# Weighting a head's values key tile by key tile for all four query tiles at once

## The chip, the cores and the metric

The kernel runs on one core of a Trainium2 chip. The metric is device time in microseconds for one execution. Three runs of the kernel before gave 3425.62, 3419.9 and 3424.49 us, median 3424.49. The profiled execution took 3425.8 us.

## The reference

Three transformer blocks over 512 tokens of width 1024, all in float32: two of the first kind (two gated feed-forwards around a mixer) and one of the second (16 meta tokens go ahead, one feed-forward). A mixer projects its input, runs attentions as branches, and merges them through gates. What the change touches is the last step of each attention, the product of the probabilities with the values:

```
p = jax.nn.softmax(sc, axis=-1)
a = p[:, :, 0] - lam * p[:, :, 1]
return jnp.einsum('bhqk,bhke->bhqe', a.astype(v.dtype), v)          # differential ("C"), 4 heads of 128
...
out = jnp.einsum('bkgnqj,bknjd->bkgnqd', p.astype(v.dtype), vb)     # sliding window ("B"), 8 heads of 64
out = jnp.einsum('bhrcij,bhrijd->bhrcd', p, vg)                     # neighbourhood ("A"), 8 heads of 64
...
o = jnp.einsum('bnhgqk,bnkhd->bnqhgd', p, v_band)                   # second block: causal window ("S")
o = jnp.einsum('bhqk,bkhd->bqhd', p, v)                             # second block: forgetting ("F")
```

Each attention is over 4 query tiles of 128 tokens. In C a query tile sees all 4 key tiles, in B its own and the neighbours, in S the one before and its own, in F all up to its own. Key tile 0 (S and F) holds the 16 meta tokens.

## The kernel before

Five programs, one for each engine, are written out by hand and meet at counted semaphores. Activations lie transposed in SBUF, weights are streamed in, split into a high and a low float32r part (`wh` by ACT, `wl` by DVE), and every dense product is three matmuls. Stages run in the order v = 0 to 7: feed-forwards at 0, 2, 3, 5 and 7, mixers at 1 and 4 (attentions C, B, A) and at 6 (S, F).

An attention (`ATT`, L427) is a list of units. Unit u is head x = u // 4 and query tile j = u % 4 + 1, with its key tiles. C has 16 units, the others 32. All engines loop over n (L1096 on TensorE, L1627 on ACT, L2342 on DVE). In round n TensorE does, in this order:

- the scores of unit n (`PS<-stk` in the rows);
- a piece of other dense work, the filler (`PS<-uh,wh` and its like), as much as the stage's quota says (`Fill`, L358, L379, L390): most rounds have one piece of six matmuls or more, in B rounds 24 and 31 have none, in F rounds 19, 21, 24, 26, 28 and 30 have none;
- `turned` (L1152): the transposes of the probabilities of unit n - lag into bank 6 or 7 (`PS<-ident,tmp`, L1171, key tile 0 at L1164). The lag is 3, in C 2. Below this is called turn u;
- `weighted` (L1174) for unit n - lag - 2: one fp32 matmul of 128 columns for each key tile, `V` as weights and the transposed probabilities `PT` as the moving operand (`PS<-PT,V`). In F units j = 1 and j = 2 go together.

DVE takes the maximum and the bias of unit n (L2297, in F L2276) and normalises unit n - 1. ACT takes the exponential of unit n (L1555) and copies turn u from PSUM to `PT` (L1588, `PT<-PS`; below: copy u). `PT` has room for the four units of one head. Where the filler's quota is zero or the attention is F, ACT makes copy u first and the exponential of unit n after it, otherwise the exponential comes first:

```
                    idle = n >= len(fill.quota) or fill.quota[n] == 0
                    if 0 <= u < A.n and (idle or st == "F"):
                        turned(v, st, u)
                    if n < A.n:
                        exponential(v, st, n)
```

The sum of a head lies in bank 3 (in B and S bank 3 or 2), from where ACT takes it after unit j = 4.

Of the kernel before, what the change touches and what calls it, by code (L numbers as in the profile page):

```python
# [15 lines left out]
P = 128  # L16
# [401 lines left out]
class Units:  # L418
# [8 lines left out]
ATT = {  # L427
    "C": Units("C", [(x, j, [1, 2, 3, 4]) for x in range(4) for j in range(1, 5)], 2, 4),
    "B": Units("B", [(x, j, [i for i in (j - 1, j, j + 1) if 1 <= i <= 4]) for x in range(8) for j in range(1, 5)], 3, 8),
    "A": Units("A", [(x, j, [1, 2]) for x in range(8) for j in range(1, 5)], 3, 8),  # L430
    "S": Units("S", [(x, j, [j - 1, j]) for x in range(8) for j in range(1, 5)], 3, 8),
    "F": Units("F", [(x, j, list(range(j + 1))) for x in range(8) for j in range(1, 5)], 3, 8),
}
# [14 lines left out]
def build(nc, T, OUT, CUM, VAL):  # L448
    JOBS, PIECES, CUTS, FILLS = plan()
    ctx = ExitStack()  # L450
    with ctx:
# [7 lines left out]
        def sb(name, shape, dt, offset):  # L459
            return nc.alloc_sbuf_tensor_at(name, list(shape), dt, offset=offset)  # L460
# [36 lines left out]
        V = sb("V", [P, 5, 512], F32, XV)  # L497
        PT = sb("PT", [P, 5, 512], F32, XV + 10240)
# [23 lines left out]
        def bank(b, c0=0, c1=512):  # L522
            return PS[:, 512 * b + c0:512 * b + c1]
# [26 lines left out]
        def slots_of(st, p):  # L550

            if st in "CAF":
                return pair_slots(p)
            return [2 * (p % 2), 2 * (p % 2) + 1], ([(4, 5), (6, 7)] if st == "B" else [(8, 9), (10, 11)])

        def pair_of(st, x):
            return (x, None) if st == "C" else (x // 2, x % 2)

        def v_cols(st, x):
            if st in "BS":  # L560
                return slice(0, P)
            return slice(P * x, P * x + P) if st == "C" else slice(P * (x // 2), P * (x // 2) + P)

        def tiles(v):
            return [0, 1, 2, 3, 4] if v == 6 else [1, 2, 3, 4]
# [4 lines left out]
        def tokens(j):  # L570
            q0 = 0 if j == 0 else X0 + P * (j - 1)
            return slice(q0, q0 + P)

        def grid(ap):

            return ap.rearrange("p (r c) -> p r c", c=64)
# [145 lines left out]
        class S:  # L722
            mm = Signal(ctx.enter_context(nc.semaphore("s_dense")))
# [3 lines left out]
            st = Signal(ctx.enter_context(nc.semaphore("s_sums")))  # L727
# [3 lines left out]
            pt = Signal(ctx.enter_context(nc.semaphore("s_probabilities_t")))  # L731
# [7 lines left out]
            x = [Signal(ctx.enter_context(nc.semaphore(f"s_x{i}"))) for i in range(8)]  # L739
# [39 lines left out]
        def tensor_program(E):  # L779
            e, held = E.e, {}  # L780

            def take(b, signal, *event):

                if b in held:
                    E.wait_ge(*held[b])
                held[b] = (signal, *event)

            def mm(out, lhs, rhs, start, stop):
                return e.matmul(out, lhs, rhs, start=start, stop=stop, skip_group_check=True)  # L789
# [306 lines left out]
            def attention(v, st, fill):  # L1096
                A = ATT[st]
                jobs = iter(fill.jobs)
                now, left = iter(()), [0]

                def filler(steps):
                    nonlocal now
                    for _ in range(steps):
                        if left[0] == 0:
                            job = next(jobs)
                            now, left[0] = dense(job, v, "o" if job.kind == "br" else "u"), job.kt // 2 * len(job.chunks)
                        next(now)
                        left[0] -= 1

                for n in range(A.n + A.lag + 4):  # L1110
                    if n < A.n:
                        x, j, kts = A.units[n]
                        p, hh = pair_of(st, x)
                        E.wait_ge(S.dv, "stk", ("q", v, st, p))
                        E.wait_ge(S.kd[0 if st in "BS" else p % 2], "halves", ("k", v, st, 0 if st in "BS" else p))
                        qs, ks = slots_of(st, p)
                        if st == "C":
                            for s in range(2):
                                b = (2, 4, 5)[(2 * n + s) % 3]
                                take(b, S.ex, "exp", v, st, n, s)  # L1120
                                scores(v, st, n, b, qs[s], *ks[s], S.sc, (st, v, n, s))
                        else:
                            b = 4 if st == "F" and j == 4 else 4 + n % 2
                            take(b, S.sx, "max", v, st, n)
                            if st == "F" and j == 4:
                                take(5, S.sx, "max", v, st, n)
                            scores(v, st, n, b, qs[hh], *ks[hh], S.sc, (st, v, n))
                    if n < len(fill.quota):
                        filler(fill.quota[n])
                    if st == "S" and n == 1:  # L1130
                        values_turned(v, "S")
                    u = n - A.lag
                    if 0 <= u < A.n:
                        turned(v, st, u)
                    u = n - A.lag - 2
                    if 0 <= u < A.n:
                        if st != "F":
                            weighted(v, st, u)
                        elif A.units[u][1] > 1:
                            for i in (u - 1, u) if A.units[u][1] == 2 else (u,):  # L1140
                                weighted(v, st, i)
                    u = n - A.lag - 4 + 1
                    if st == "C" and 0 <= u < A.n and A.units[u][1] == 4:
                        x = A.units[u][0]
                        b = 6 + u % 2
                        take(b, S.an, "c_sum", v, x)
                        E.wait_ge(S.an, "c_out", v, x)
                        for q in range(4):
                            i = mm(bank(b, q, q + 1), oblf[:, x, X0 + P * q:X0 + P * q + P], ones[:, 0:1], True, True)
                        i.then_inc(*S.st.up(("c_sum", v, x)))  # L1150

            def turned(v, st, u):  # L1152

                A = ATT[st]
                x, j, kts = A.units[u]
                E.wait_ge(S.id, "id")
                E.wait_ge(S.ex if st == "F" else S.sx, "p", v, st, u)
                b = 6 + u % 2
                take(b, S.pt, "pt", v, st, u)
                if 0 in kts:  # L1160
                    b0, c0 = (6 + u % 2, 384) if st == "S" else (2, 0)
                    if st == "F":
                        take(2, S.pt, "pt0", v, st, u)
                    i = e.transpose(bank(b0, c0, c0 + P)[0:16, :], scores_of(st, u, 0, 16), ident[:, :])  # L1164
                    i.then_inc(*S.tp.up(("pt0", v, st, u)))
                for a in kts:
                    if a > 0:
                        k0, k1 = key_range(a)
                        if st == "A":
                            k0, k1 = P * (a - 1), P * a  # L1170
                        i = e.transpose(bank(b, P * (a - 1), P * a), scores_of(st, u, k0, k1), ident[:, :])  # L1171
                i.then_inc(*S.tp.up(("pt", v, st, u)))

            def weighted(v, st, u):  # L1174

# [110 lines left out]
        def scalar_program(E):  # L1286
# [301 lines left out]
            def turned(v, st, u):  # L1588

                A = ATT[st]  # L1590
                x, j, kts = A.units[u]
                if u >= len(A.units) // (4 if st == "C" else 8):
                    E.wait_ge(S.pv, st, v, u - len(A.units) // (4 if st == "C" else 8))
                big = [i for i in kts if i > 0]
                b = 6 + u % 2
                if 0 in kts:
                    b0, c0 = (b, 384) if st == "S" else (2, 0)
                    E.wait_ge(S.tp, "pt" if st == "S" else "pt0", v, st, u)
                    E.wait_ge(S.dv, "zero")
                    act(PT[0:16, 0, P * (j - 1):P * j], bank(b0, c0, c0 + P)[0:16, :], ACT.Copy).then_inc(  # L1600
                        *S.pt.up(("pt0", v, st, u)))
                a, z = big[0], big[-1] + 1
                to = 2 if st == "A" else 0
                E.wait_ge(S.tp, "pt", v, st, u)
                act(PT[:, a + to:z + to, P * (j - 1):P * j],
                    bank(b, P * (a - 1), P * (z - 1)).rearrange("p (i q) -> p i q", q=P), ACT.Copy).then_inc(
                    *S.pt.up(("pt", v, st, u)))
# [1344 lines left out]
```

## Time and profile before

| | us |
|---|---|
| median of three runs | 3424.49 |
| profiled execution | 3425.8 |
| its span, first to last instruction | 3423.9 |
| TensorE busy in the span | 3348.1 |
| VectorE busy | 2413.3 |
| ScalarE busy | 1687.4 |
| TensorE clock granted, share of full speed | 0.996 |

The span is almost all TensorE. A matmul's record in the trace covers its way through the array, and records overlap, so that the rate of a series is read from the starts or from the length of a whole series, not from one record's length. An fp32 matmul has two records (the 592 products of probabilities with values give 1184), a float32r matmul one.

### The profile page before, as it was taken

How to read it: one execution, taken by the hardware profiler on the slowest of the kernel's cores; microseconds unless marked ns; L12 is line 12 of the kernel's file. 1: busy time of each engine (PE TensorE's matmuls, PEld its weight loads, DVE VectorE, ACT ScalarE, POOL GpSimd, SP SyncE). 2: the span in 40 equal slices, each digit the busy share in tenths (PEclk: the TensorE clock that was granted, in tenths of full speed). 3: DMA queues.
4: the chain of work that ended last, by engine and by line, in shares of the span. 5: the costliest groups of instructions: out<-in, count | busy, mean ns of one | idle time of the engine just before them, and what ended most of it. 6: DMA issues, size and time to landing. Idle time of an engine off the chain costs nothing.

```text
span 3423.9 us, 51537 instructions
## 1 busy us (share of the span) xinstructions
PE 3348.1 (98%) x20344; PEld 2954.7 (86%) x20344; DVE 2413.3 (70%) x3919; ACT 1687.4 (49%) x3057; POOL 816.6 (24%) x607
## 2 busy tenths in 40 slices
PE   8999999999999999999999999999999999999998
PEld 6999887878889998999887878889988888888997
DVE  6878665756687778777766656687768676649775
ACT  4545454635454445445454544454446374334443
POOL 1533110121043413432111021053400001205331
PEclk9999999999999999999999999999999999999999
DMA  3333343253223332333433253223322322322332
GB/s 130 108 96 110 104 107 84 69 142 90 86 93 102 102 106 74 105 105 112 109 82 93 69 148 93 74 92 102 109 95 91 90 79 69 111 84 85 102 107 81
DMA packets 116673, 332.79 MB, mean 97 GB/s; under 512 B 18888, under 2 KB 19656, under 8 KB 116432
## 3 DMA queue, kind: packets, MB, share of 16 engines
q1 hardware_dynamic: 104112, 306.82, 28.9%
q0 software_dynamic: 12320, 22.66, 3.3%
q8 instruction: 162, 2.65, 0.3%
q14 instruction: 79, 0.65, 0.1%
HBM read 306.23 MB, written 4.21 MB: 91 GB/s over the span
## 4 chain that ended last, share of the span: by engine, by line
PE 84%; DVE 9%; ACT 2%; DMA 2%; issue 1%; POOL 1%; SPq 0%; DVEq 0%; POOLq 0%; ACTq 0%
PE PS L789 82%; DVE wl L1839 2%; PE PS L1171 2%; DVE bl L2023 1%; ACT wh L1290 1%; DMA raw<-in_gu 1%; DVE gx L1987 1%; DMA raw<-in_win 1%; POOL ws L2700 0%; DVE bf L2003 0%; DVE tmp L1911 0%; DVE tmp L1968 0%; DVE h L1914 0%; DVE b L2003 0%; DVE b L2004 0%
## 5 line engine op out<-in xcount | busy, mean ns | idle before, releaser
L1839 DVE TENSOR_TENSOR wl<-raw,wh 128x1024 fp32r<-128x1024 f32 (+2 forms) x635 | 790.9, 1249 | 300.0 <-ACT wh L1290 293.3
L1290 ACT ACTIVATE wh<-raw 128x1024 fp32r<-128x1024 f32 (+2 forms) x635 | 553.9, 878 | 413.5 <-PE PS L789 387.6
L789 PE MATMUL PS<-bh,wh 128*128 128x256 f32 x2520 | 710.1, 282 | 6.8 <-DVE h L1936 2.9
L789 PE MATMUL PS<-bh,wl 128*128 128x256 f32 x2520 | 708.0, 281 | 0.0
L789 PE MATMUL PS<-bl,wh 128*128 128x256 f32 x2520 | 707.9, 281 | 0.0
L789 PE MATMUL PS<-uh,wh 128*128 128x512 f32 (+2 forms) x1656 | 616.4, 372 | 24.0 <-DVE ul L1867 16.2
L789 PE MATMUL PS<-uh,wl 128*128 128x512 f32 (+2 forms) x1656 | 606.6, 366 | 0.0
L789 PE MATMUL PS<-ul,wh 128*128 128x512 f32 (+2 forms) x1656 | 604.6, 365 | 0.0
L789 PEld LDWEIGHTS PS<-bh,wh 128*128 128x128 f32 x2520 | 474.8, 188 | 11.6 <-DVE h L1936 3.3
L789 PEld LDWEIGHTS PS<-bh,wl 128*128 128x128 f32 x2520 | 474.8, 188 | 0.6
L789 PEld LDWEIGHTS PS<-bl,wh 128*128 128x128 f32 x2520 | 474.9, 188 | 0.0
L789 PE MATMUL PS<-gx,wh 128*128 128x512 f32 (+1 forms) x1424 | 429.3, 375 | 14.6 <-DVE gx L1987 11.9
L789 PEld LDWEIGHTS PS<-uh,wh 128*128 128x128 f32 x1656 | 313.1, 189 | 82.0 <-DVE wl L1839 15.3
L789 PEld LDWEIGHTS PS<-ul,wh 128*128 128x128 f32 x1656 | 313.3, 189 | 52.4
L789 PEld LDWEIGHTS PS<-uh,wl 128*128 128x128 f32 x1656 | 313.1, 189 | 47.3 <-issue 1.4
L789 PEld LDWEIGHTS PS<-gx,wh 128*128 128x128 f32 x1424 | 261.2, 189 | 69.4 <-DVE gx L1987 14.1
L1839 DVE TENSOR_TENSOR wl<-ws,wh 128x1024 fp32r<-128x1024 f32 x180 | 269.2, 1496 | 34.7 <-ACT wh L1290 34.7
L789 PE MATMUL PS<-gx,wl 128*128 128x512 f32 (+1 forms) x712 | 266.5, 374 | 0.0
L2700 POOL TENSOR_TENSOR ws<-raw 128x512 f32<-128x512 f32 x90 | 124.7, 1386 | 537.4 <-DMA raw<-in_gu 304.7
L1290 ACT ACTIVATE wh<-ws 128x1024 fp32r<-128x1024 f32 x180 | 191.0, 1061 | 114.1 <-PE PS L789 83.4
L1290 ACT ACTIVATE tmp<-PS 128x256 f32<-128x256 f32 (+1 forms) x382 | 146.8, 386 | 161.3 <-PE PS L789 161.0
L2726 POOL DMA_DIRECT2D tmp<-tmp x88 | 69.6, 1324 | 586.3 <-DVE tmp L2230 456.2
(263 smaller groups left out, 5693.7 us busy)
## 6 DMA issues: line engine op xcount, KB each, us to landing
raw<-in_gu SPq DMA_DIRECT2D x220, 512.0 KB, 3.2
raw<-in_win SPq DMA_DIRECT2D x139, 512.0 KB, 3.3
raw<-in_dn SPq DMA_DIRECT2D x80, 320.0 KB, 3.0
raw<-in_dn SPq DMA_DIRECT2D x40, 512.0 KB, 3.6
raw<-in_wbr SPq DMA_DIRECT2D x72, 256.0 KB, 2.7
raw<-in_wout SPq DMA_DIRECT2D x24, 512.0 KB, 3.2
raw<-in_dn SPq DMA_DIRECT2D x40, 256.0 KB, 2.7
raw<-in_wv SPq DMA_DIRECT2D x20, 512.0 KB, 3.2
```

Source lines behind the costliest of these rows:

```text
L789: return e.matmul(out, lhs, rhs, start=start, stop=stop, skip_group_check=True)
L1171: i = e.transpose(bank(b, P * (a - 1), P * a), scores_of(st, u, k0, k1), ident[:, :])
L1290: return e.activation(out, in_, f, scale=scale, **more)
L1839: tt(wl[:, c % 4, 0:n], src, wh[:, c % 4, 0:n], SUB).then_inc(*S.lo.up(("lo", c)))
L1987: tt(lo, tmp[:, 2 + f % 2, X0:TW], hi, SUB).then_inc(*S.dv.up(("g", v, f)))
L2023: tt(bl[:, i, :], b21[:, :] if i == 2 else bf[:, i, :], bh[:, i, :], SUB).then_inc(*S.dn.up(("operand", v, i)))
L2700: tt(ws[:, 0:512], b[:, 0:512], b[:, 512:1024], ADD).then_inc(*S.pl.up(("sum1", p)))
L2726: e.dma_start(tmp[o:o + 32, temp_of(tag), X0:TW], turn_at(turn_of(tag))[a:a + 32, X0:TW], accum_op=ADD).then_inc(*S.rp[turn_of(tag)].land( ...
```

## The change

For every head but the last of C, B, S and F, the products are no longer made unit by unit. A new function `weighted_head` runs once per head, in the round in which the next head's first unit is turned, ahead of that turn. It waits for all four copies of the head and makes one matmul for each key tile, over all query tiles that see it: 4 matmuls of 512 columns in C; of 256, 384, 384 and 256 in B; of 128, 256, 256, 256 and 128 in S; of 512, 512, 384, 256 and 128 in F. On ACT a copy into `PT` waits for the whole head that lay there. Attention A and the last heads are as before.

```diff
@@ -571,6 +571,14 @@
             q0 = 0 if j == 0 else X0 + P * (j - 1)
             return slice(q0, q0 + P)
 
+        def together(st, x):
+
+            return st != "A" and x < ATT[st].units[-1][0]
+
+        def weighed(v, st, u):
+
+            return st, v, u | 3 if together(st, ATT[st].units[u][0]) else u
+
         def grid(ap):
 
             return ap.rearrange("p (r c) -> p r c", c=64)
@@ -1130,10 +1138,12 @@
                     if st == "S" and n == 1:
                         values_turned(v, "S")
                     u = n - A.lag
+                    if 0 < u < A.n and A.units[u - 1][1] == 4 and together(st, A.units[u - 1][0]):
+                        weighted_head(v, st, u - 1)
                     if 0 <= u < A.n:
                         turned(v, st, u)
                     u = n - A.lag - 2
-                    if 0 <= u < A.n:
+                    if 0 <= u < A.n and not together(st, A.units[u][0]):
                         if st != "F":
                             weighted(v, st, u)
                         elif A.units[u][1] > 1:
@@ -1170,6 +1180,29 @@
                             k0, k1 = P * (a - 1), P * a
                         i = e.transpose(bank(b, P * (a - 1), P * a), scores_of(st, u, k0, k1), ident[:, :])
                 i.then_inc(*S.tp.up(("pt", v, st, u)))
+
+            def weighted_head(v, st, u):
+
+                A = ATT[st]
+                x, units = A.units[u][0], A.units[u - 3:u + 1]
+                vc = v_cols(st, x)
+                for t in (tiles(v) if st in "CF" else tiles(v)[-4:][:1] + tiles(v)[:-4]):
+                    E.wait_ge(S.aa, "vv", v, st, t)
+                for i in range(u - 3, u + 1):
+                    if 0 in A.units[i][2]:
+                        E.wait_ge(S.pt, "pt0", v, st, i)
+                    E.wait_ge(S.pt, "pt", v, st, i)
+                b = 3 if st in "CF" else (3, 2)[x % 2]
+                if st == "C":
+                    take(b, S.an, "c_out", v, x)
+                else:
+                    take(b, S.dv, "ol", v, st, x)
+                keys = sorted({a for unit in units for a in unit[2]})
+                for a in keys:
+                    js = [j for _, j, kts in units if a in kts]
+                    c0, c1 = P * (js[0] - 1), P * js[-1]
+                    i = mm(bank(b, c0, c1), V[:, a, vc], PT[:, a, c0:c1], a == keys[0], a == keys[-1])
+                i.then_inc(*S.pv.up((st, v, u)))
 
             def weighted(v, st, u):
 
@@ -1589,8 +1622,8 @@
 
                 A = ATT[st]
                 x, j, kts = A.units[u]
-                if u >= len(A.units) // (4 if st == "C" else 8):
-                    E.wait_ge(S.pv, st, v, u - len(A.units) // (4 if st == "C" else 8))
+                if u >= 4:
+                    E.wait_ge(S.pv, *weighed(v, st, u - 4))
                 big = [i for i in kts if i > 0]
                 b = 6 + u % 2
                 if 0 in kts:
```

The first head of B, TensorE, rounds 7 and 8 (`PS<-ident,tmp` is turn 4, `PS<-stk` the scores of unit 8). Before:

```order
L789 MATMUL PS<-ul,wh 128x512
L1171 MATMUL PS<-ident,tmp 128x128 [waits s_probabilities_t,s_softmax]
L1171 MATMUL PS<-ident,tmp 128x128
L789 MATMUL PS<-PT,V 128x128 x3
L789 MATMUL PS<-stk 128x256 [waits s_softmax,s_dve_dense]
```

and now:

```order
L797 MATMUL PS<-ul,wh 128x512
L797 MATMUL PS<-PT,V 128x256 [waits s_probabilities_t]
L797 MATMUL PS<-PT,V 128x384 x2
L797 MATMUL PS<-PT,V 128x256
L1181 MATMUL PS<-ident,tmp 128x128 [waits s_softmax]
L1181 MATMUL PS<-ident,tmp 128x128
L797 MATMUL PS<-stk 128x256 [waits s_softmax,s_dve_dense]
```

The product of the head stands ahead of turn 4 and waits for copy 3 (`s_probabilities_t`), which was made one round earlier.

The end of B, TensorE, rounds 31 to 34 (scores of unit 31, turns 28, 29 and 30). Before:

```order
L789 MATMUL PS<-stk 128x256 [waits s_softmax]
L789 MATMUL PS<-stk 128x256
L1171 MATMUL PS<-ident,tmp 128x128 [waits s_probabilities_t,s_softmax]
L1171 MATMUL PS<-ident,tmp 128x128
L789 MATMUL PS<-PT,V 128x128 x3
L1171 MATMUL PS<-ident,tmp 128x128 [waits s_probabilities_t,s_softmax]
L1171 MATMUL PS<-ident,tmp 128x128 x2
L789 MATMUL PS<-PT,V 128x128 x2
```

and now:

```order
L797 MATMUL PS<-stk 128x256 [waits s_softmax]
L797 MATMUL PS<-stk 128x256
L797 MATMUL PS<-PT,V 128x256 [waits s_dve_dense,s_probabilities_t]
L797 MATMUL PS<-PT,V 128x384 x2
L797 MATMUL PS<-PT,V 128x256
L1181 MATMUL PS<-ident,tmp 128x128 [waits s_softmax]
L1181 MATMUL PS<-ident,tmp 128x128
L1181 MATMUL PS<-ident,tmp 128x128 [waits s_softmax]
L1181 MATMUL PS<-ident,tmp 128x128 x2
```

Four matmuls of head 6 now stand between the last scores and turn 28; what was weighted after turns 28 and 29 is gone from there.

## Rows read from the trace of the kernel before

**Rows 1.** The page's first part: busy time, share of the span, instructions.
```profile
PE 3348.1 (98%) x20344; PEld 2954.7 (86%) x20344; DVE 2413.3 (70%) x3919; ACT 1687.4 (49%) x3057; POOL 816.6 (24%) x607
```
**Rows 2.** Timeline of TensorE: start us, length us, operation, records; fp32 series only.
```profile
484.66 0.95 PE L789 MATMUL PS<-ones,oblf 128*128 128x1 f32 x8
...
530.06 2.84 PE L789 MATMUL PS<-PT,V 128*128 128x128 f32 x24
...
546.22 1.02 PE L789 MATMUL PS<-tmp,ones 128*128 128x512 f32 x2
```
**Rows 3.** Busy time by window: B of v = 1, S and F.
```profile
597.00:680.00 83.00, 80.02 (x489) 69.77 (x488) 65.68 (x215) 55.84 (x151) 10.73 (x14) 1.00 0.26 70
...
2588.00:2663.00 75.00, 74.59 (x457) 63.99 (x456) 61.62 (x222) 53.95 (x166) 3.23 (x6) 1.00 0.24 78
2728.00:2832.00 104.00, 100.81 (x684) 89.78 (x683) 74.71 (x164) 72.13 (x185) 3.22 (x6) 1.00 0.29 87
```
**Rows 4.** Timeline of TensorE, B of v = 1.
```profile
605.56 0.38 PE L1171 MATMUL PS<-ident,tmp 128*128 128x128 f32 x2
...
608.09 0.38 PE L1171 MATMUL PS<-ident,tmp 128*128 128x128 f32 x2
...
610.36 0.51 PE L789 MATMUL PS<-stk 128*128 128x256 f32 x2 [1.23 <-DVE stk L2248]
...
655.44 0.38 PE L1171 MATMUL PS<-ident,tmp 128*128 128x128 f32 x2
...
671.95 0.38 PE L1171 MATMUL PS<-ident,tmp 128*128 128x128 f32 x2
...
673.08 0.38 PE L1171 MATMUL PS<-ident,tmp 128*128 128x128 f32 x2
...
677.51 0.41 PE L1171 MATMUL PS<-ident,tmp 128*128 128x128 f32 x2 [1.76 <-ACT PT L1290]
```
**Rows 5.** Timeline of ACT, the same stage: copies 3, 19, 27, 28, exponential 31, copy 29.
```profile
608.93 0.36 ACT L1290 ACTIVATE PT<-PS 128x256 f32<-128x256 f32 x1
...
655.02 0.36 ACT L1290 ACTIVATE PT<-PS 128x256 f32<-128x256 f32 x1
...
672.41 0.36 ACT L1290 ACTIVATE PT<-PS 128x256 f32<-128x256 f32 x1
673.56 0.38 ACT L1290 ACTIVATE PT<-PS 128x256 f32<-128x256 f32 x1 [0.79 <-PE PS L1171]
674.00 0.51 ACT L1290 ACTIVATE tmp<-tmp,small 128x256 f32<-128x256 f32 x1
...
676.89 0.47 ACT L1290 ACTIVATE PT<-PS 128x384 f32<-128x384 f32 x1
```
**Rows 6.** Timelines in S: turn 12, copy 11, DVE ahead of it.
```profile
2621.20 0.27 PE L1164 MATMUL PS<-ident,tmp 128*16 128x128 f32 x1
...
2620.84 0.36 ACT L1290 ACTIVATE PT<-PS 128x256 f32<-128x256 f32 x1
...
2618.01 1.39 DVE L2248 TENSOR_TENSOR stk<-tmp,stk 64x512 fp32r<-64x512 f32 x2
```
**Rows 7.** Timeline of TensorE in F: turns 12, 16, 20 and 24.
```profile
2782.11 0.27 PE L1164 MATMUL PS<-ident,tmp 128*16 128x128 f32 x1
...
2792.53 0.27 PE L1164 MATMUL PS<-ident,tmp 128*16 128x128 f32 x1
...
2802.98 0.27 PE L1164 MATMUL PS<-ident,tmp 128*16 128x128 f32 x1
...
2812.51 0.27 PE L1164 MATMUL PS<-ident,tmp 128*16 128x128 f32 x1
```
**Rows 8.** Timeline of ACT in F: copies 19, 23 and 27.
```profile
2800.18 0.73 ACT L1290 ACTIVATE PT<-PS 16x128 f32<-16x128 f32 x2
...
2809.64 0.72 ACT L1290 ACTIVATE PT<-PS 16x128 f32<-16x128 f32 x2
...
2818.72 0.73 ACT L1290 ACTIVATE PT<-PS 16x128 f32<-16x128 f32 x2
```

## The prediction

> **What bounds the kernel now.** I read the page's first part: TensorE is busy 3348.1 us of a span of 3423.9, DVE 70%, ACT 49% [rows 1]. So TensorE sets the time, and what counts is its own work and each moment at which it stands still. Then the windows of the stages that change [rows 3]: in B, S and F TensorE is busy 96%, 99% and 97%, DVE 79%, 82% and 72%, ACT 67%, 72% and 69%. Hardly any stall is there to be won back; a new one is paid in full. Last the timelines around each head's end [rows 4 to 8], for how soon after a turn ACT's copy is ready, since the head's product now waits for the copy one round earlier.
>
> **TensorE's own work.** Before, a series of 24 records of 128 columns is 2.84 us long, a record on its own 0.275: (2.84 - 0.275) / 23 = 0.1115 us a record. One column costs nearly as much: 8 records in 0.95 us, so about 0.10 each. Two records of 512 columns last 1.02 us, one alone 0.592: 0.428 us apart, and 0.428 is 3.84 times 0.1115, not once [rows 2]. So at 128 columns the streaming has all but caught up with the weight load, and a wide matmul saves next to nothing.
>
> Moved are C 6 heads x 16, B 14 x 10, S 7 x 8 and F 7 x 14 matmuls: 390, or 780 records of 128 columns, 87.0 us. New are 150 matmuls. Widths of 256 and 384 are not in the trace as fp32. Bounds: by columns from the 512 row 0.214 and 0.321, by whole 128-column records 0.223 and 0.335. I take 0.216 and 0.322, near the 512 row, as the steps are the same streaming. 38 matmuls of 512 x 2 x 0.428 = 32.5; 35 of 384: 22.5; 56 of 256: 24.2; 21 of 128: 4.7; together 83.9 us. The change saves 3.1 us of TensorE, 1.5 to 3.3 by the bounds. A head's product lasts 3.4 us in C, 2.15 in B, 1.74 in S, 3.0 in F.
>
> For the narrow matmul the Trainium skill ("TensorE: Matmul & The Clock Gate", Back-to-back issue gap) gives a stream of weight loads and matmuls about 81 ns at 128 columns and 131 ns at 512, that is, the load weighs most and width is cheap. By its ratio, 131/81 x 0.1115 = 0.18 us for a 512 record, the estimated saving would be some 40 us, not 3; the trace's 0.428 disagrees.
>
> **The wait that is added, B.** The product of head x needs copy 4x + 3, and everything behind it on TensorE waits with it: turn, scores, filler. TensorE also comes to it sooner, for the products of units before are gone.
> Head 0: turn 3 starts at 605.56 and turn 4 at 608.09; without units 0 and 1 (4 and 6 records, 1.1 us) TensorE would be ready for the product at 607.1 on the old time line. Copy 3 is done at 608.93 + 0.36 = 609.29, as ACT first stacks a query (which waits for a DMA), converts weights and takes the exponential; from a copy's end to TensorE's start 0.15 us pass (676.89 + 0.47 to 677.51) [rows 4, 5]. Stall 2.3 us. The stall of 1.23 at 610.36 goes, its data being there at 610.3 and the scores now later. Net +1.0.
> Head 4: ready at 655.44 less units 15 to 17 (14 records, 1.56) = 653.9; copy 19 ends at 655.38, and can come at most 0.45 earlier, as ACT runs on without a gap there: stall 1.2 us. Head 2 by the same working 0.2. Heads 1, 3 and 5 have their copies ready well ahead (1.3 to 1.7 us before the turn) and stall nothing; their rows, which repeat the pattern, are not shown, here and for the heads named without rows below. The end of B: round 31 has no filler. Turn 27 is at 671.95, its copy over at 672.77, so the product of head 6 starts 0.97 us after the turn and ends at +3.12; turn 28 follows, copy 28 0.48 later, and only then the exponential of unit 31, for in this round ACT copies first: at +4.0. It was at 674.00, +2.05. Everything to the end of B hangs on this exponential: TensorE already waits 1.76 us for copy 29 [rows 4, 5]. So +2.0, and no product left to fill the gap. Sum per layer: 1.0 + 0.2 + 1.2 + 2.0, less six heads' saving 0.47 and less unit 24 (0.45), which the old program has behind it at turn 27 and the new one not: +3.5. Two layers (v = 1 and 4, whose copies lie alike): +7.0 us.
>
> **S.** Always one filler, so exponential first. Turn 12 at 2621.20, copy 11 over at 2621.20, behind DVE, which is busy without a gap since it stacked the next query (2618.01) and cannot hurry [rows 6]. Without units 7 to 9 (12 records, 1.34 us) TensorE is ready at 2619.86, so it stalls 1.5 us. Head 4 has the same pattern, 1.5; head 0 has 0.75; heads 1, 3, 5 and 6 none. The saving is 0.3. The end of S is bound by ACT's copies, and the old program at turn 28 still had units 26 and 27 (0.9 us) to put beside them: 3.75 - 0.3 + 0.9 = +4.3 us.
>
> **F.** ACT always copies first, so the exponential waits through the whole product of the last head. Up to turn 12 the quotas are 2 and 3 and hide it: at turn 12 the new program has made units 10 and 11 too (18 records, 2.0 us), less 0.3 saved: +1.7, to be kept, since from here ACT sets the pace. From turn 20 (2802.98) copy 23 ends 7.38 later (2810.36) with ACT never idle between copy 20 and it; the product then takes 3.0, and turn 24 comes at +10.5 where it came at +9.53: +1.0. From turn 24 copy 27 ends at +6.94, 0.37 of it spare: +9.7 for 8.9, +0.7. From 12 to 16 (10.42) I get +0.75, from 16 to 20 (10.45) nothing, TensorE being last there (copy 19 ends 2800.91) [rows 7, 8]. The tail is ACT's as before. Sum +4.2 us.
>
> **C.** Rounds last 5 to 6 us and copies are ready 3.8 us and more ahead; the rates save 0.4 us a layer, the tail, which is a chain over ACT, gives back the unit 11 that filled it (0.9), and ACT's output comes 0.3 earlier: +0.2 a layer, +0.4.
>
> **Sum.** 7.0 + 4.3 + 4.2 + 0.4 = +15.9 us, on 3425.8 (span and 1.9 around it): 3441.7. The median shown lies 1.3 below the profiled run: 3440. After each attention TensorE goes on with dense work at once, with nothing to absorb this.
>
> **Rivals.**
> 1. The chains give way: DVE and ACT follow TensorE forward where it comes sooner, stalls inside B and S vanish, and only the structural parts stay: the end of B (2.0 less 0.9, twice), F about 2.5, S 0.6. Sum about +6: 3430. For it: DVE is only 82% busy even in S. Against: it is without a gap just ahead of copy 11.
> 2. Not slower, on the other side: the two-round distance was not needed, copies keep ready and the wide matmuls' 3.1 us is all: 3421. It holds if copy 3 and copy 11 end before TensorE is there; against it stand 609.29 and 2621.20. A variant, that weight loads alone set the pace and a record of any width costs the one-column 0.10: 780 x 0.1115 less 300 x 0.10, -57 us, 3367; the 0.428 row rules it out.
> 3. Worse: TensorE's work comes in lumps, so DVE idles through each product and then has 1.88 us a round (61.62 over the window's 33 rounds of 2.29) against TensorE's shortened 1.84 in S; new waits for weights and maxima in every head, 0.5 us in each of 28 heads: +14 on top, 3454.
>
> **Chances.** Forecast 0.55 (own range 3435 to 3446), rival 1 0.2, rival 2 0.09 and its cheap variant 0.01, rival 3 0.15. 0.2% is 6.8 us, about what a measurement can tell. Rival 2 lies within it, rival 1 on its edge (3431.3), half either way: same 0.19, faster 0.01, and 0.80 slower, of which I move 0.01 to faster. The range 3427 to 3450 leaves out the fast cases and the heavy end of rival 3.
>
> **What would show it.** `PS<-PT,V` of 512 columns 0.43 us apart. TensorE idle ahead of `PS<-PT,V` waiting for ACT's `PT`: about 2.3 us at head 0 of B, 1.2 at head 4, 1.5 at heads 2 and 4 of S, 0.5 in late F. At the end of B the exponential of unit 31 some 4 us after turn 27. B's window longer by 3.5 us each, S's by 4.3, F's by 4.2, A's and the feed-forwards' the same. The prediction is wrong if these stalls are absent, or if copies end sooner than on the old time line; and in its sum if 256- and 384-column records are not near 0.22 and 0.32 us.

## The result, and the profile after

The changed kernel takes 3448.38 us, the median of four runs (3443.92 to 3454.84), beside 3424.56 for the kernel before (3419.9 to 3425.62). The ratio is 1.0067, 95% interval 1.0055 to 1.0079: slower by 0.67%. The prediction was 3440, range 3427 to 3450. Five later executions of the same kernel had a median of 3451.61 (below, "The changed kernel again"). The profiled execution of the changed kernel took 3454.84 us, at a mean granted TensorE clock of 0.992; that of before had 0.996.

The page's first part, changed kernel: TensorE has 480 records fewer, as 390 matmuls became 150, and yet is busy 12.5 us longer than in [rows 1]. The lower clock can account for that: leaving out the stretch in which each program ends, this execution has 44 us at half clock and the one of the kernel before has 17, and half of the 27 us between them is 13.6.

```profile
PE 3360.6 (97%) x19864; PEld 2931.0 (85%) x19864; DVE 2420.1 (70%) x3919; ACT 1686.7 (49%) x3057; POOL 813.2 (24%) x607
```

The waits of TensorE, changed kernel (engine, what waited and where, what for: us in all, times, longest). Before, the first of these lines did not reach 1 us, and the other two were 6.7 us (4 times) and 2.4 us (3 times).

```profile
PE PS L797 <- ACT PT L1323: 11.7, 11, 2.5
PE PS L1181 <- ACT PT L1323: 9.1, 8, 2.3
PE PS L1174 <- ACT PT L1323: 6.9, 8, 2.0
```

Together 27.7 us of standing still for ACT's copies where there were 9.4: 18 us more, of which products not left to fill the old waits are a part. (The 9.4 hold 0.3 us of the first line.)

TensorE's timeline, attention B of v = 1, changed kernel (start, length, operation, records, in brackets the idle time before it and its releaser). It answers to [rows 4]: turn 3, the product of head 0, turn 4; the product of head 4 and turn 20; turn 27, the product of head 6, turns 28 and 29, turn 31.

```profile
605.89 0.38 PE L1181 MATMUL PS<-ident,tmp 128*128 128x128 f32 x2
...
610.44 3.77 PE L797 MATMUL PS<-PT,V 128*128 128x256 f32 x8 [2.50 <-ACT PT L1323]
614.05 0.38 PE L1181 MATMUL PS<-ident,tmp 128*128 128x128 f32 x2
...
658.94 2.39 PE L797 MATMUL PS<-PT,V 128*128 128x256 f32 x8 [1.04 <-ACT PT L1323]
661.17 0.38 PE L1181 MATMUL PS<-ident,tmp 128*128 128x128 f32 x2
...
675.82 0.38 PE L1181 MATMUL PS<-ident,tmp 128*128 128x128 f32 x2
...
676.91 2.39 PE L797 MATMUL PS<-PT,V 128*128 128x256 f32 x8 [0.47 <-ACT PT L1323]
679.13 0.71 PE L1181 MATMUL PS<-ident,tmp 128*128 128x128 f32 x5
...
683.39 0.41 PE L1181 MATMUL PS<-ident,tmp 128*128 128x128 f32 x2 [2.29 <-ACT PT L1323]
```

ACT's, the end of the same stage; it answers to the last rows of [rows 5].

```profile
676.45 0.36 ACT L1323 ACTIVATE PT<-PS 128x256 f32<-128x256 f32 x1
679.61 0.38 ACT L1323 ACTIVATE PT<-PS 128x256 f32<-128x256 f32 x1 [2.81 <-PE PS L1181]
679.89 0.50 ACT L1323 ACTIVATE tmp<-tmp,small 128x256 f32<-128x256 f32 x1
...
682.78 0.47 ACT L1323 ACTIVATE PT<-PS 128x384 f32<-128x384 f32 x1
```

The product waits 2.50 us at head 0 (2.3 forecast) and 1.04 at head 4 (1.2). The exponential of unit 31 starts 4.07 us after turn 27 (679.89 less 675.82; forecast 4.0, before 2.05), with ACT idle 2.81 ahead of copy 28.

Below, a stage's price is the start of its last turn against its first one, less the same of the kernel before (in a few lines the end of the last copy is taken). Changed kernel: C +0.1 and +0.1; B +5.1 (v = 1) and +4.1 (v = 4); A nothing; S +4.5; F +8.5. The +5.1 and +8.5 hold a stretch at the lower clock. The first begins at 609.8, behind the 2.50 us for which TensorE stood still. Windows of the changed kernel (busy us and instructions of TensorE, its weight loads, DVE, ACT, POOL; granted clock; DMA), and of this stretch in the kernel before:

```profile
609.80:613.20 3.40, 2.76 (x5) 1.85 (x6) 2.78 (x9) 1.28 (x5) 0.00 (x0) 0.50 0.47 154
2828.50:2831.90 3.40, 3.40 (x9) 2.31 (x8) 1.89 (x5) 1.14 (x3) 0.00 (x0) 0.50 0.00 0
```

```profile
609.80:613.20 3.40, 2.84 (x17) 2.53 (x18) 2.98 (x13) 1.88 (x8) 0.00 (x0) 1.00 0.46 154
```

0.50 is the lower of the two levels, 1.2 GHz. It costs half of the time for which TensorE works in it. In the second stretch that is half of 3.4 us, 1.7. In the first TensorE still stood for 0.6 us: from its start to turn 4 the product took 3.61 us where the product of head 4 took 2.23, so the stretch cost 1.4. Without these two the stages add up to 0.2 + 3.7 + 4.1 + 4.5 + 6.8 = 19.3 us, and the prediction had 15.9. Two things were left to find: F, 2.6 us dearer than forecast, and some 4.5 us between 19.3 and the measured 23.8. (The expectations below were worked out with 1.7 for the first stretch, +3.4 for B of v = 1 and 19.2 for the sum.)

### The profile page after: what moved, and what is told of

The parts are those of the page before. It is cut to its first block, busy times and chain, and to the rows that moved or that the text cites. A ratio compares the mean times of both kernels' runs of the same rounds, so it can differ in the third digit from the quotient of the medians.

```text
span 3453.0 us, 50525 instructions
## 1 busy us (share of the span) xinstructions
PE 3360.6 (97%) x19864; PEld 2931.0 (85%) x19864; DVE 2420.1 (70%) x3919; ACT 1686.7 (49%) x3057; POOL 813.2 (24%) x607
## 4 chain that ended last, share of the span: by engine, by line
PE 83%; DVE 10%; ACT 3%; DMA 2%; issue 1%; POOL 1%; SPq 0%; DVEq 0%; ACTq 0%; POOLq 0%
PE PS L797 81%; DVE wl L1872 2%; PE PS L1181 1%; DVE bl L2056 1%; DMA raw<-in_gu 1%; ACT wh L1323 1%; DMA raw<-in_win 1%; ACT tmp L1323 1%; DVE gx L2020 1%; DVE bf L2036 0%; DVE tmp L2001 0%; DVE tmp L1944 0%; DVE h L1947 0%; DVE b L2036 0%; DVE b L2037 0%
## 5 line engine op out<-in xcount | busy, mean ns | idle before, releaser
L797 PE MATMUL PS<-bh,wh 128*128 128x256 f32 x2520 | 710.9, 282 | 5.7 <-DVE h L1969 2.9
L797 PE MATMUL PS<-bh,wl 128*128 128x256 f32 x2520 | 708.7, 281 | 0.0
L797 PE MATMUL PS<-bl,wh 128*128 128x256 f32 x2520 | 708.6, 281 | 0.0
L797 PE MATMUL PS<-uh,wh 128*128 128x512 f32 (+2 forms) x1656 | 618.6, 374 | 25.5 <-DVE ul L1900 16.8
L797 PE MATMUL PS<-uh,wl 128*128 128x512 f32 (+2 forms) x1656 | 607.7, 367 | 0.0
L797 PE MATMUL PS<-ul,wh 128*128 128x512 f32 (+2 forms) x1656 | 605.9, 366 | 0.0
L797 PEld LDWEIGHTS PS<-bh,wh 128*128 128x128 f32 x2520 | 475.5, 189 | 10.1 <-DVE h L1969 3.3
L797 PEld LDWEIGHTS PS<-bh,wl 128*128 128x128 f32 x2520 | 475.6, 189 | 0.6
L797 PEld LDWEIGHTS PS<-bl,wh 128*128 128x128 f32 x2520 | 475.7, 189 | 0.0
L797 PE MATMUL PS<-gx,wh 128*128 128x512 f32 (+1 forms) x1424 | 430.3, 376 | 13.3 <-DVE gx L2020 11.9
L797 PEld LDWEIGHTS PS<-uh,wh 128*128 128x128 f32 x1656 | 313.9, 190 | 83.9 <-DVE wl L1872 15.9
L797 PEld LDWEIGHTS PS<-ul,wh 128*128 128x128 f32 x1656 | 314.2, 190 | 53.1
L797 PEld LDWEIGHTS PS<-uh,wl 128*128 128x128 f32 x1656 | 314.1, 190 | 47.3 <-issue 1.4
L797 PEld LDWEIGHTS PS<-gx,wh 128*128 128x128 f32 x1424 | 261.9, 190 | 68.1 <-DVE gx L2020 14.1
L797 PE MATMUL PS<-gx,wl 128*128 128x512 f32 (+1 forms) x712 | 267.1, 375 | 0.0
```

## The experiments

Each ran in several rounds beside the kernel before (median 3425.5 us in the first and third series, 3422.93 in the second). The theory: the price is the stages' own, from the place of the product (its wait for copy 4x + 3, and the product missing where TensorE waits later on), while width gives 3.1 us back. Rivals: the wide matmuls themselves are slow; the loss is the clock's; each lump costs in every head.

**One attention alone.** The rule that picks the heads is cut to one attention (here B; the others with "S" and "F"):

```
-            return st != "A" and x < ATT[st].units[-1][0]
+            return st == "B" and x < ATT[st].units[-1][0]
```

> The change in attention B alone; C, S and F weight unit by unit as before. Theory (the stages pay each for themselves, by the stalls in front of the heads' products and at the end of the attention): the turns of B move by +3.4 in v = 1 and +4.05 us in v = 4 (the trace of the changed kernel, without its half-clock stretch), so +7 to +9 us on 3424.6: 3432 to 3434. Rival (the loss is one of the whole: the stages carry it on, or it comes through the granted clock, which more stretches at half speed take down): less than +4 us here, or well over +10. In the trace the theory wants 11 to 12 us for the whole wait of PS<-PT,V for ACT's PT less what C, S and F had of it, some 7 us, and S and F as in the kernel before.

> The change in attention S alone. Theory: +4.3 to +4.5 us (stalls of 1.5, 1.5 and 0.75 us in front of heads 4, 2 and 0, and the lost cover at the end): 3429. Rival: the loss is not of this stage: within 1.5 us of 3424.6. B and F as in the kernel before.

> The change in attention F alone. The prediction gave +4.2 us; the trace of the changed kernel has +6.8 without its half-clock stretch and +8.5 with it. Theory (ACT's copy ahead of the exponential, and turns that wait for the bank which the key tile 0 of the turn before still fills): +6 to +9 us, 3431 to 3433. Rival (the extra of F was handed on from B and S, or was the clock's): +4.2 or less, 3428.8.

Measured: B alone 3437.05 us, ratio 1.0026 (1.0016 to 1.0036); S alone 3429.11, 1.0007 (0.9998 to 1.0015); F alone 3435.78, 1.0025 (1.0016 to 1.0034). In the traces B costs +3.3 in v = 1 and +5.2 in v = 4. The latter again has 1.7 us of the lower clock at head 0, where the product works through all of the stretch (3.92 us to turn 4 for 2.23): +3.5. S costs +4.5. F costs +7.0 with no such stretch in it, so its extra was neither handed on nor the clock's. Stages without the change keep their length within 0.25 us. 3.3 + 3.5 + 4.5 + 7.0 + 0.2 = 18.5 us: the stages pay each for themselves. In device time S alone can't be told from no change, as its interval holds 1; its price is read from the trace. The medians of B and F alone lie 3 to 5 us above what their stages explain; this is taken up with the clock, below.

**Place against width.**

```
-                for a in keys:
-                    js = [j for _, j, kts in units if a in kts]
-                    c0, c1 = P * (js[0] - 1), P * js[-1]
-                    i = mm(bank(b, c0, c1), V[:, a, vc], PT[:, a, c0:c1], a == keys[0], a == keys[-1])
+                for _, j, kts in units:
+                    c0, c1 = P * (j - 1), P * j
+                    for a in kts:
+                        i = mm(bank(b, c0, c1), V[:, a, vc], PT[:, a, c0:c1], a == kts[0], a == kts[-1])
```

> The products stand where the changed kernel has them, with its waits, but each head is weighted unit by unit with matmuls of 128 columns (780 records instead of 300). It tells the place from the width. Theory (the place costs, and width saves 780 x 0.1115 - 83.9 = 3.1 us): 3.1 us above the changed kernel, about 3447 to 3451.5, 6.5 to 8 per thousand above the kernel before. Rival W (the wide matmuls are what is slow): 10 us or more below the changed kernel, 3434 or less. Rival C (the granted clock falls more often because the product is shorter and stalls come sooner after it): as the changed kernel or faster by the stretches at half clock, of which it would have fewer.

Measured: 3451.51 us, ratio 1.0069 (1.0057 to 1.0081), as slow as the changed kernel or a little slower. Timeline of TensorE, the product of head 4 of B in this kernel:

```profile
658.69 2.47 PE L797 MATMUL PS<-PT,V 128*128 128x128 f32 x20 [1.01 <-ACT PT L1322]
661.00 0.38 PE L1181 MATMUL PS<-ident,tmp 128*128 128x128 f32 x2
```

From the product's start to the turn are 2.31 us in narrow matmuls and 2.23 (658.94 to 661.17) in wide ones. By stage, with 1.7 us taken off for each stretch at 0.5, the narrow kernel costs C +0.5, B +3.8 and +4.0, S +4.9, F +7.1. The wide one costs 0.4 a layer less in C, 0.3 in S and in F. In B the totals are nearly the same, but there the stall at head 0 was shorter by 0.4 and 0.6 us in the narrow kernel's trace; from turn 4 on the wide one gains 0.4 and 0.5. That makes a little over 2 us in all. Width helps, and hardly; the place costs. The medians alone would not show the 2 us: the intervals of the two kernels overlap. The wide matmuls as culprit (3434 or less) are out.

**Behind the turn, or a round later.**

```
-                    if 0 < u < A.n and A.units[u - 1][1] == 4 and together(st, A.units[u - 1][0]):
-                        weighted_head(v, st, u - 1)
                     if 0 <= u < A.n:
                         turned(v, st, u)
+                    if 0 < u < A.n and A.units[u - 1][1] == 4 and together(st, A.units[u - 1][0]):
+                        weighted_head(v, st, u - 1)
```

and for the second kernel, where the changed kernel has the call for unit u - 1 (cut to the new lines):

```
+                    if 1 < u < A.n and A.units[u - 2][1] == 4 and together(st, A.units[u - 2][0]):
+                        weighted_head(v, st, u - 2)
```

> All as in the changed kernel, but the head's product stands behind turn 4x + 4 instead of ahead of it. Theory (the loss is the wait for copy 4x + 3 and the turn kept behind the product): the product is wanted one turn later (0.4 to 0.9 us), so the stalls of head 0 and 4 in B and of heads 0, 2, 4 in S shrink by 0.4 to 0.5 each and the turn itself is not late; at the end of B turn 28 and exponential 31 are not held by product 6 except through copy 28, which overwrites the head's PT and waits for it anyway. In all 3 to 6 us below the changed kernel, 3442 to 3445. Rival (copy 4x + 4 waits for the product in any case, so nothing is won): 3448, as the changed kernel.

> All as in the changed kernel, but the head's product stands one round later, ahead of turn 4x + 5: as far behind copy 4x + 3 as the last unit of a head was before. Theory: the stalls in front of the products go in B (2.3 and 1.2 us less the 1.23 of the old stall) and in S (1.5 + 1.5 + 0.75), the ends stay, and ACT's copy 4x + 4, which overwrites the head's PT, now waits a round for the product; behind it in rounds with filler nothing hurries, in F the exponential does. 6 to 12 us below the changed kernel, 3436 to 3442, with C, B and S near the kernel before and F still +5 or more. Rival (the wait only moves: copy 4x + 4 comes later by what the product was moved, and turn 4x + 6, which needs its bank, stalls instead): 3447 to 3452.

Behind the turn: 3447.36 us, ratio 1.0061 (1.0047 to 1.0075), so no gain that can be measured. Its stages, with 1.7 taken off where a whole stretch at 0.5 lies in them, are C 0.1 twice, B 2.7 and 2.9, S 3.6, F 6.4: some 3.5 us less than in the changed kernel, at the low end of what was expected. The stall at head 0 of B is 2.27 instead of 2.50, as the turn fills only what it is long:

```profile
606.63 0.38 PE L1181 MATMUL PS<-ident,tmp 128*128 128x128 f32 x2
609.28 4.11 PE L797 MATMUL PS<-PT,V 128*128 128x256 f32 x8 [2.27 <-ACT PT L1323]
```

A round later: 3480.08 us, ratio 1.0156 (1.0139 to 1.0172). The theory failed here, and its rival was too mild as well. The waits of ACT's copies for TensorE (for a product L797, for a turn L1181), first in this kernel, then in the changed one:

```profile
ACT PT L1323 <- PE PS L797: 145.3, 34, 10.3
ACT PT L1323 <- PE PS L1181: 64.9, 53, 3.2
```

```profile
ACT PT L1323 <- PE PS L1181: 135.4, 94, 5.3
```

With the waits for key tile 0 (L1174) these are 218 us here, 170 in the changed kernel and 122 in the kernel before. A copy that waits for a product (PS L797) is copy 4x + 4, which overwrites the head's `PT`; it does so 34 times, once for 10.30 us, in C:

```profile
476.67 0.60 ACT L1323 ACTIVATE PT<-PS 128x512 f32<-128x512 f32 x1 [10.30 <-PE PS L797]
```

Behind it stand ACT's exponentials and weight conversions. C costs +6.0 and +4.7, B +7.1 twice, S +3.9, F +19.5; of these 48 us stretches at 0.5 are about 9. The stalls ahead of the early products are gone, as expected (at turn 8, B of v = 4 stands at +0.8 and S at -0.9), but what ACT loses is more. In F TensorE then waits 10.4 us for ACT's copies at the turns of key tile 0, where it waited 6.9 in the changed kernel and 2.4 before. `PT` holds one head, so where ACT's copies are late the product can neither wait for the last copy at no price nor be late for the next one.

**F: the order on ACT, and the early heads alone.**

```
-                    if 0 <= u < A.n and (idle or st == "F"):
+                    if 0 <= u < A.n and idle:
```

(and in the second condition likewise); and, from the changed kernel, `return st == "F" and x < 4`.

> All as in the changed kernel, but in the rounds of F that have filler ACT takes the exponential ahead of the copy, as in B and S. Theory (F's 7.0 us come from exponentials and scales that are held behind a copy which waits for the product): 2 to 4 us below the changed kernel, 3444 to 3446, and ACT's idle time in heads 4 to 6 (5.1 us at head 5) less than half. Rival (the copies themselves are what F waits for, and they now come 1 us later in every round): 2 to 6 us above it, 3450 to 3455.

> The change in F alone and there in heads 0 to 3 only; heads 4 to 6, C, B and S are weighted unit by unit as before. Theory (F's loss is made in heads 4 to 6, where ACT sets the pace up to turn 4x + 3, and then scores, filler and the whole product follow one another on TensorE): up to turn 16 as in the changed kernel (+2.1, of which 1.7 is work done early, given back by turn 20), and the stage at +0.5 to +1 instead of +7.0: 3425 to 3427. Rival (the loss begins in the early heads and is only seen late): +3 us or more for the stage.

With the exponential first: 3446.41 us, ratio 1.0065 (1.005 to 1.0079). ACT's idle time ahead of copy 24 falls to 1.36 us from the 3.5 that the clean trace below has, as expected, but F costs +6.4 by its last turn, against +7.0 in F alone: not the 2 to 4 us less, and not more either. Both readings fail for the stage as a whole. By its parts neither is empty: up to turn 20 this order is 1.4 us behind that of F alone (+4.1 for +2.7), and it wins back 0.4 us by turn 24, 0.3 by turn 28 and 1.2 behind it. So the order on ACT moves time within F, and nearly nothing is left of it in the sum.

Heads 0 to 3 alone: 3425.93 us, ratio 1.0005 (0.9995 to 1.0016). Against the kernel before, F's turns stand at +1.9 at turn 4, +2.0 at turn 16, +0.10 at turn 20 and +0.12 at turn 31; its last copy ends 0.6 later, with 1.8 us of a stretch at 0.5 just ahead. So F's price is made in heads 4 to 6, with fillers short or missing there: in the trace of F alone 1.0, 2.4 and 1.9 us, and the 1.7 of work done early, which it does not get back. How, is in the trace of F alone, head 5 (turns 20 to 23, the scores of unit 27, the product, turn 24; between scores and product lies the filler of six `uh` and `ul` matmuls):

```profile
2801.41 0.27 PE L1174 MATMUL PS<-ident,tmp 128*16 128x128 f32 x1
...
2802.19 0.27 PE L1174 MATMUL PS<-ident,tmp 128*16 128x128 f32 x1 [0.22 <-ACT PT L1323]
...
2804.69 0.27 PE L1174 MATMUL PS<-ident,tmp 128*16 128x128 f32 x1 [0.36 <-ACT PT L1323]
...
2807.14 0.27 PE L1174 MATMUL PS<-ident,tmp 128*16 128x128 f32 x1 [1.48 <-ACT PT L1323]
...
2808.15 0.96 PE L797 MATMUL PS<-stk 128*128 128x16 f32 x4 [0.30 <-DVE tmp L2309]
...
2810.34 3.18 PE L797 MATMUL PS<-PT,V 128*128 128x512 f32 x10
2813.35 0.27 PE L1174 MATMUL PS<-ident,tmp 128*16 128x128 f32 x1
```

and ACT's copies 23 and 24 beside it:

```profile
2808.08 0.73 ACT L1323 ACTIVATE PT<-PS 16x128 f32<-16x128 f32 x2
...
2813.72 0.42 ACT L1323 ACTIVATE PT<-PS 16x128 f32<-16x128 f32 x2 [3.52 <-PE PS L1174]
```

Turn 23 comes 5.73 us after turn 20, and before it was 5.72 (turn 23 at 2808.70, turn 20 in [rows 7]): the head lasts as long in both kernels up to there. But the old one had 18 records of products in that stretch, and 10 behind turn 23, and stood still for only 0.38 us in it, ahead of turn 23. The new one has none of them, and its turns wait for ACT's copy of the turn before, since every turn of F puts its key tile 0 into bank 2: it stands still for 0.22 + 0.36 + 1.48 + 0.30 = 2.4 us. Then follow, one behind the other, turn 23 with its scores and filler (2807.14 to 2810.34, 3.2 us) and the product (3.0). Turn 24 is at +11.94, where it was at +9.53 and where the forecast had +10.5. The product doesn't wait for its copy at all (copy 23 is over at 2808.81), while ACT idles 3.52 us and DVE 2.90 us through it. For head 6 the same: turns 24 to 28 take 10.77 us, before 8.92. This is read from the trace; no kernel was run in which the product stands ahead of the filler.

**The end of B.** In b_not_6 head 6 is left to `weighted` (`x < 6` for B). In b_exp31_first ACT, in round 31 of B, takes the exponential first and copy 28 right after it:

```
+                    last = st == "B" and n == A.n - 1
-                    if 0 <= u < A.n and (idle or st == "F"):
+                    if 0 <= u < A.n and (idle or st == "F") and not last:
                         turned(v, st, u)
                     if n < A.n:
                         exponential(v, st, n)
+                    if last:
+                        turned(v, st, u)
... (the second condition, behind the filler's work, gets `or last`)
```

> All as in the changed kernel, but head 6 of B is weighted unit by unit as before, so only heads 0 to 5 are taken at once. It prices the end of B, which the prediction put at +2.0 for the exponential of unit 31 behind copy 28 and +0.45 for unit 24. Theory: 2.4 us less in each of two layers, less 0.08 for the wide matmuls: 4.7 us below the changed kernel, 3443.7. Rival (the end is bound by ACT's copies whatever the product does): within 1 us of it, 3448.

> All as in the changed kernel, but at the end of B ACT takes the exponential of unit 31 ahead of copy 28, for which it idles 2.81 us. Theory (everything to the end of B hangs on this exponential, which came 2.0 us later than before): B shorter by 1.5 to 2.0 us in each of two layers, 3 to 4 us below the changed kernel. Rival (the copies and ACT's other work behind it set the end): less than 0.5 us a layer.

b_not_6: 3445.49 us, ratio 1.0062 (1.0048 to 1.0076). From turn 24 to turn 31 its B gains 1.1 us on the kernel before in each layer, and the changed kernel loses 0.45: the end is worth 1.55, not 2.4. The expectation had a sign wrong. Unit 24's 0.45 us is work that the changed kernel no longer has at the end, so by the prediction's own terms the end costs 2.0 - 0.45 = 1.55, and that is what was found. Its ratio can't be told from the changed kernel's, so this price too is the trace's. b_exp31_first: 3446.78, ratio 1.0059 (1.0047 to 1.0071), and every one of its five times lies below every one of the changed kernel's five in the same series (3444.39 to 3447.18 against 3449.69 to 3453.3). Between turns 28 and 31 it gains 1.5 us a layer, where the order of the changed kernel gains 0.17: 1.3 less for one line moved on ACT. Its timelines, first ACT (exponential 31, copies 28 and 29), then TensorE (turn 31):

```profile
674.91 0.51 ACT L1323 ACTIVATE tmp<-tmp,small 128x256 f32<-128x256 f32 x1 [0.39 <-DVE small L2335]
...
677.33 0.38 ACT L1323 ACTIVATE PT<-PS 128x256 f32<-128x256 f32 x1 [1.63 <-PE PS L1181]
...
679.17 0.48 ACT L1323 ACTIVATE PT<-PS 128x384 f32<-128x384 f32 x1
```

```profile
679.80 0.41 PE L1181 MATMUL PS<-ident,tmp 128*128 128x128 f32 x2 [0.97 <-ACT PT L1323]
```

The wait ahead of turn 31 falls from 2.29 to 0.97 us. It does not go, since copy 29 stands behind a weight conversion (1.05 us) and the scaling of `stkf` (0.71 us). So the exponential behind copy 28 was the mechanism, and worth 1.3 of the 2.0.

**Only heads whose copies are ready.**

```
-            return st != "A" and x < ATT[st].units[-1][0]
+            return (st, x) in READY_HEADS
```

`READY_HEADS` holds heads 0 and 1 of C and F, and heads 1, 3 and 5 of B and S.

> Only such heads are weighted at once as have their copies ready in the trace of the kernel before and are neither in an end of an attention nor in the late part of F: heads 0 and 1 of C and F, heads 1, 3 and 5 of B and S. Theory (a stall-free head costs nothing and saves the 0.26 us of C, 0.07 of B, 0.03 of S and 0.1 of F that the rates give): 2 x 2 x 0.13 + 2 x 3 x 0.07 + 0.1 + 0.1 = about 1 us below the kernel before at an equal clock, which can't be told from no change; C, B, S and F each within 0.5 us of their length before. Rival (every head costs 0.5 us or more, by the lumps): 16 heads, +5 us or more, 3430.

Measured: 3423.17 us, ratio 0.9986 (0.9974 to 0.9998). By stage: C -0.2 twice, B +0.1 and -0.1, S -0.1, F -0.2, some 0.8 us less in all, about what was forecast. The interval just leaves out 1, but the traces hold only a part of its middle, so this is at best a gain of a few hundredths of a per cent, and may be none. The rival, a loss in every head, is out. It is the best of the versions run.

**The changed kernel again.**

> The changed kernel once more, beside more runs of the kernel before. The stages' own prices add to 0.2 (C) + 3.4 and 4.05 (B) + 4.5 (S) + 7.0 (F) = 19.2 us at an equal granted clock. Theory (the rest is the clock's, whose mean over the runs of the changed kernel was 0.9930 against 0.9948 before, at some 2.4 us for each 0.001): ratio 1.0060 to 1.0075 and a mean clock of 0.9925 to 0.994. Rival (the lower clock was chance, four runs being few): mean clock 0.9945 or more and a ratio of 1.0056 or less.

Measured: 3451.61 us, median of five, ratio 1.0074 (1.0062 to 1.0086), mean clock 0.9926, both as expected. Each run has its granted clock. Of the kernel before there are 58: with a mean clock of 0.993 the median is 3429.3 us, 0.994: 3428.0, 0.995: 3424.4, 0.996: 3422.8, 0.997: 3419.5; so 0.001 went with some 2.4 us. The mean clock was 0.9947 before, 0.9928 over nine runs of the changed kernel: 0.0019 / 0.001 x 2.4 = 4.6 us. This is an estimate: at one clock the runs still spread, those of the changed kernel at 0.993 from 3444.84 to 3451.62 (16 to 22 us above 3429.3), and one run of before took 3447.01 at 0.994. The same holds for the first series, means against the mean of its own 24 runs of before (3426.0 us at 0.9945): B alone is 9.8 us above it with a clock 0.0010 lower, so 7.4 at an equal clock, and its stages have 6.8; F alone 9.0 and 0.0010, so 6.6, stage 7.0; S alone 2.6 with a clock 0.0007 higher, so 4.3, stage 4.5. The stages and the clock together make 19.3 + 4.6 = 23.9 us; the two medians of the changed kernel lie 23.8 and 26.1 above those of before. The 2 us more of the second series have no term.

## Why the prediction held, and where it was off

The time was forecast at 3440 and came at 3448, within the range, slower as said, and by the mechanism given: the new wait for the last copy of a head, and no products left for the waits that follow. It lies near the range's upper end, and the second series, with 3451.61, just outside it; that the first median fell inside is in part the luck of its four runs. Of the 7.9 us by which 15.9 fell short of 23.8, F has 2.6 to 2.8, the clock an estimated 4.6 and B 0.8. By its steps:

- **The rates.** Held. In C the product of 8 records of 512 columns is 3.60 us long, one alone 0.60: 3.00 / 7 = 0.429 a record (0.428 forecast):

```profile
516.62 3.60 PE L797 MATMUL PS<-PT,V 128*128 128x512 f32 x8
```

  In the product of head 4 of B the starts of the records are 0.216 us apart at 256 columns and 0.322 at 384, as forecast. To the turn behind it, B's product takes 2.23 us for 2.15. The forecast saving, 3.1, is a little over 2 in the narrow kernel's comparison. The ratio that the Trainium skill gives for a stream of weight loads and matmuls ("TensorE: Matmul & The Clock Gate", Back-to-back issue gap), by which a 512 record would be an estimated 0.18 us, has the trace against it again.
- **B, +3.5 a layer.** Held: +3.3 to +4.1 over the traces, with stalls of 2.50 and 1.04 us at heads 0 and 4, and the end at 1.55. (At head 0 a small slip is in the forecast: 608.09 less 1.1 is 607.0, not 607.1, which makes its stall 2.4 to 2.5.) The spread is there by turn 4: the stall at head 0 lies between 2.0 and 2.7 us in the traces, as copy 3 stands behind a query that waits for a DMA.
- **S, +4.3.** Held: +4.5. The turns stand at +1.7, +3.1 and +4.5 at turns 4, 12 and 20. Less the 0.9 us of products done early, heads 0, 2 and 4 cost 0.8, 1.4 and 1.4; the trace of the changed kernel has stalls of 0.59, 1.27 and 1.21 us ahead of their products (0.75, 1.5, 1.5 forecast). At head 2:

```profile
2633.20 1.98 PE L797 MATMUL PS<-PT,V 128*128 128x128 f32 x10 [1.27 <-ACT PT L1323]
```

- **C, +0.2.** Held, +0.1 a layer.
- **F, +4.2.** This term was mis-sized: it is 7.0 in F alone, 6.8 in the changed kernel. Up to turn 12 it is right (+1.7), and so is the sum of the next two heads (+1.0 for 0.75). The failing step is "from turn 20 copy 23 ends 7.38 later ... the product then takes 3.0, and turn 24 comes at +10.5". It let the product follow the copy. The copy came as forecast, at +7.40. But on TensorE the scores of unit 27 and the filler stand between turn 23, which ACT holds at +5.7, and the product, so the start is at 5.73 + 3.20 = +8.93, not +7.38. Heads 5 and 6 cost 2.4 and 1.9 where 1.0 and 0.7 were forecast.
- **The clock.** It was in no term. The nine runs have an estimated 4.6 us of it, more than any error in a stage.
- **The rivals.** "The chains give way" (3430): B and S kept their stalls (2.50, 1.04 and 1.27 us). "Not slower" (3421) fell with them. "Worse, 0.5 us in each of 28 heads" (3454) hit a time near the measured one by a mechanism that isn't there: heads 1, 3 and 5 of B and S cost nothing when they alone were gathered.

## What to carry to other kernels

When small products are gathered into one, ask first what gaps they filled: here they ran in waits of TensorE that stayed when they were gone. Then follow each engine's whole queue up to the gathered piece, since it can be late by its own engine's queue, as in F, and not only by its data, as in B and S. And before widening matmuls, take the time of a record at two widths from the trace: if it grows nearly as the columns do, there is nothing to gain. Gather only where the data is ready before the engine, which now comes sooner, gets there (heads 1, 3 and 5 of B, whose copies were over 1.3 to 1.7 us ahead of the next turn), and where no other engine sets the pace of the rounds (not in late F).

## What the runs showed of the hardware

The granted clock differed between runs of one kernel (0.993 to 0.997), in single stretches at its lower level. Leaving out the stretch in which each program ends, the profiled execution of the kernel before had five such stretches of 3.4 us (0.996) and that of the changed kernel eleven, two of them 6.8 us long (0.992), some in stages that the change leaves alone. Eight profiled executions had a stall of 2.0 to 2.7 us at head 0 of B in both layers; right behind it the clock was at 0.5 in 8 of these 16 places, and in the kernel before in neither. Over the series the mean clock was lower where B or F were changed (0.9936, 0.9935) and not for S alone (0.9953) or F's early heads (0.9954), beside 0.9945 before in the same series; that these two lie 0.0008 and 0.0009 above it is explained by nothing in these kernels, so differences of this size may be chance. That the stalls bring it is argued from this, not shown; no kernel was run with stalls alone.
